# A transformer block of eight stages on one core: the order of the last products of a stage, of the first products of the next, and of a weight split between them

## What is computed

```python
# first block
x = x + g1 * short_conv_mixer(modulate(rmsnorm(x, norm1_g), sh1, sc1), ...)
x = x + g2 * swiglu(modulate(rmsnorm(x, norm2_g), sh2, sc2), ffn_w_in, ffn_w_out)
x = rmsnorm(x, final_g)
# second block, for l in 0, 1
h = _swiglu(_rmsnorm(x, g[0]), w_gate[l, 0], w_up[l, 0], w_down[l, 0])
x = x + 0.5 * _rmsnorm(h, g[1])
h = _rmsnorm(x, g[2])
h = _mixer_even(h, ...) if l % 2 == 0 else _mixer_odd(h, ...)   # conv + window attention / forgetting attention
x = x + _rmsnorm(h, g[3])
h = _swiglu(_rmsnorm(x, g[4]), w_gate[l, 1], w_up[l, 1], w_down[l, 1])
x = x + 0.5 * _rmsnorm(h, g[5])
```

## Time and profile before

| | us |
|---|---|
| median of 3 runs (lowest, highest) | 1375.23 (1374.13, 1375.32) |
| profiled execution, whole | 1372.25 |
| its span, first to last instruction | 1370.5 |
| TensorE busy (share) | 1292.2 (94%) |
| VectorE busy | 832.8 (61%) |
| ScalarE busy | 670.5 (49%) |
| GpSimd busy | 156.8 (11%) |
| mean granted TensorE clock | 0.988 of full |

### The profile page before, as it was taken

How to read it: one execution, slowest core, us unless ns; L and a number is a source line. 1 busy time by engine, 2 the same in 40 slices (tenths; PEclk the granted TensorE clock), 3 DMA queues, 4 the chain that set the end, 5 groups by cost and what they waited for, 6 DMA issues and landing times.

```text
span 1370.5 us, 18389 instructions
## 1 busy us (share of the span) xinstructions
PE 1292.2 (94%) x6757; PEld 1079.7 (79%) x6757; DVE 832.8 (61%) x1015; ACT 670.5 (49%) x993; POOL 156.8 (11%) x121
## 2 busy tenths in 40 slices
PE   2969899999899999899999999999999999999997
PEld 1859688888688888786788888888888798788886
DVE  5998664454655555755655556655555577655554
ACT  2304444444555445555644456654445665644453
POOL 1880393000600000200000000000000100000000
PEclk9989999999999999999999999999999999999999
DMA  9967565555255556371465555555563433365551
GB/s 341 346 229 266 189 230 194 188 184 200 93 185 189 191 191 225 102 234 63 138 218 184 184 199 184 183 186 184 184 214 123 154 140 123 118 220 184 184 199 61
DMA packets 171452, 253.62 MB, mean 185 GB/s; under 512 B 9657, under 2 KB 135821, under 8 KB 171405
## 3 DMA queue, kind: packets, MB, share of 16 engines
q1 hardware_dynamic: 168208, 244.33, 52.7%
q0 software_dynamic: 2304, 8.41, 1.6%
q10 hardware_dynamic: 894, 0.25, 0.1%
HBM read 249.76 MB, written 1.05 MB: 183 GB/s over the span
## 4 chain that ended last, share of the span: by engine, by line
PE 84%; DVE 10%; ACT 3%; issue 1%; DMA 1%; POOL 0%; DVEq 0%; SPq 0%; ACTq 0%; POOLq 0%
PE ps L514 26%; PE ps L516 26%; PE ps L515 26%; DVE tmp L1572 2%; PE ps L556 2%; DVE w_lo L1369 2%; PE ps L816 1%; DVE x_sb L1425 1%; DVE tmp L1522 1%; DVE tmp L1420 1%; PE ps L534 1%; PE ps L711 1%; DMA raw<-in_ada_w 1%; PE ps L700 1%; ACT xn L1010 1%
## 5 line engine op out<-in xcount | busy, mean ns | idle before, releaser
L514 PE MATMUL ps<-w_lo,xT_hi 128*128 128x512 f32 x944 | 376.3, 399 | 4.8 <-DVE xT_lo L1450 2.7
L516 PE MATMUL ps<-w_hi,xT_lo 128*128 128x512 f32 x944 | 369.9, 392 | 0.0
L515 PE MATMUL ps<-w_hi,xT_hi 128*128 128x512 f32 x944 | 369.3, 391 | 0.0
L1369 DVE TENSOR_TENSOR w_lo<-raw,w_hi 128x2048 fp32r<-128x2048 f32 x117 | 278.0, 2378 | 150.0 <-ACT w_hi L988 150.0
L1374 DVE SCALAR_TENSOR_TENSOR w_lo<-raw,par,w_hi 128x512 fp32r<-128x512 f32 x336 | 230.4, 747 | 139.7 <-ACT w_hi L993 139.6
L988 ACT ACTIVATE w_hi<-raw 128x2048 fp32r<-128x2048 f32 x117 | 223.5, 1912 | 179.1 <-PE ps L516 154.3
L993 ACT ACTIVATE w_hi<-raw,par 128x512 fp32r<-128x512 f32 x336 | 214.4, 711 | 0.8 <-PE ps L516 0.8
L514 PEld LDWEIGHTS ps<-w_lo,xT_hi 128*128 128x128 f32 x944 | 178.6, 189 | 42.2 <-DVE xT_lo L1450 3.0
L516 PEld LDWEIGHTS ps<-w_hi,xT_lo 128*128 128x128 f32 x944 | 178.0, 189 | 38.2
L515 PEld LDWEIGHTS ps<-w_hi,xT_hi 128*128 128x128 f32 x944 | 178.5, 189 | 35.6 <-issue 0.2
L514 PE MATMUL ps<-w_lo,hT_hi 128*128 128x512 f32 x400 | 156.5, 391 | 0.0
(11 more groups left out here) (212 smaller groups left out, 1388.6 us busy)
## 6 DMA issues: line engine op xcount, KB each, us to landing
raw<-in_ffn_w_gate SPq DMA_DIRECT2D x88, 512.0 KB, 3.7
raw<-in_ffn_w_up SPq DMA_DIRECT2D x88, 512.0 KB, 4.7
raw<-in_ffn_w_down SPq DMA_DIRECT2D x88, 512.0 KB, 4.0
raw<-in_ffn_w_in SPq DMA_DIRECT2D x44, 512.0 KB, 4.5
raw<-in_conv_w_in SPq DMA_DIRECT2D x24, 512.0 KB, 5.1
raw<-in_fox_w_in SPq DMA_DIRECT2D x24, 512.0 KB, 4.6
raw<-in_ffn_w_out SPq DMA_DIRECT2D x22, 512.0 KB, 4.0
raw<-in_ada_w SPq DMA_DIRECT2D x16, 512.0 KB, 6.7
```

The lines of the kernel that those rows point to most:

```text
L514: pe.matmul(o, a_hi, b_lo, start=first, stop=False, skip_group_check=True)
L515: pe.matmul(o, a_hi, b_hi, start=False, stop=False, skip_group_check=True)
L516: return pe.matmul(o, a_lo, b_hi, start=False, stop=last, skip_group_check=True)
L1369: dve.tensor_tensor(w_lo[:, slot_of(n), :], raw[:, slot_of(n), :], w_hi[:, slot_of(n), :].bitcast(F32), ALU.subtract).then_inc(raw_done, 1)
```

## The change

It has six parts.
1. **Last products**: first tokens go through the last two units, then second tokens (all FFN stages, AB; in CONV over units 14 and 15, with the row product behind them; in FOX half of unit 14 for second tokens stays ahead of unit 15 for first tokens).
2. **First products** (`first_units`, `fresh_hi`, `fresh_lo`): for each unit the eight matmuls with high x come first and wait for ScalarE alone, then the four with low x. The second tokens are transposed after the high products of unit n + 1. In FFN stages both transposes use banks 2 and 3 (`turn_bank`), so the second one waits for the low part of the first.
3. **The late split** (`quarter`) is issued on ScalarE behind the root of the first tokens, and on VectorE behind the first residual.
4. **Fillers**: `WARM_NORMED` is 6 and stands only ahead of AB and FOX; all others go.
5. **Table load** of the square root after AB and FOX: earlier on ScalarE.
6. After FFN0 the final norm (`final_x`) is a step of its own; at FFN0 the wait for the shift row moves to its use.

The diff, cut to its core (ScalarE's and VectorE's lists are shown for the borders only):

```diff
-WARM_TURNED, WARM_FOLDED, WARM_FINAL, WARM_NORMED = 4, 5, 12, 18
+WARM_NORMED = 6
...
+        def turn_bank(s, t, h):
+            return 2 + h if s in FFNS else 2 * t + h
...
+                    if s in FFNS and t == 1:
+                        pe.wait_ge(xT_ok, 4 * s + h + 1)
...
+            def fresh_hi(s, n, h, t, bank):
+                hi, lo = unit(n)
+                pe.wait_ge(xT_hi_ok, 4 * s + 2 * t + h + 1)
+                for k in range(4):
+                    c = slice(k * 512, (k + 1) * 512)
+                    x_k = xT_hi[:, 4 * h + k, tok(t)]
+                    pe.matmul(ps[:, bank, :], x_k, lo[:, c], start=h == 0 and k == 0, stop=False, skip_group_check=True)
+                    pe.matmul(ps[:, bank, :], x_k, hi[:, c], start=False, stop=False, skip_group_check=True)
+            def fresh_lo(s, n, h, t, bank):
+                hi, _ = unit(n)
+                pe.wait_ge(xT_ok, 4 * s + 2 * t + h + 1)
+                for k in range(4):
+                    mm = pe.matmul(ps[:, bank, :], xT_lo[:, 4 * h + k, tok(t)], hi[:, k * 512:(k + 1) * 512], start=False,
+                                   stop=h == 1 and k == 3, skip_group_check=True)
+                return mm
+            def first_units(s, banks):
+                n = BASE[s]
+                turn_x(s, 0)
+                fresh_hi(s, n, 0, 0, banks[0])
+                fresh_lo(s, n, 0, 0, banks[0])
+                fresh_hi(s, n + 1, 1, 0, banks[0])
+                turn_x(s, 1)
+                mm = fresh_lo(s, n + 1, 1, 0, banks[0])
+                if s in FFNS:
+                    mm.then_inc(up_tok0, 1)
+                fresh_hi(s, n, 0, 1, banks[1])
+                fresh_lo(s, n, 0, 1, banks[1]).then_inc(w_used, 1)
+            def second_unit(s, bank):
+                fresh_hi(s, BASE[s] + 1, 1, 1, bank)
+                fresh_lo(s, BASE[s] + 1, 1, 1, bank).then_inc(w_used, 1)
...
-                down_part(last - 1, hT_hi, hT_lo, 0, 1, False, False).then_inc(w_used, 1)
                 pe.wait_ge(hT_ok, NCH * (f + 1))
                 down_part(last, yT_hi, yT_lo, 0, 0, False, True).then_inc(y_tok0, 1)
+                down_part(last - 1, hT_hi, hT_lo, 0, 1, False, False).then_inc(w_used, 1)
                 down_part(last, yT_hi, yT_lo, 0, 1, False, True).then_inc(w_used, 1)
...
-            for i in range(4):
+            for i, tk in ((0, 0), (0, 1), (1, 0), (1, 1), (2, 0), (3, 0), (2, 1), (3, 1)):
...
+            out_part(14, 1, ks=(0,))
             out_part(15, 0)
+            out_part(14, 1, ks=(1,))
             out_part(15, 1)
... ScalarE, in between(b)
-                if b not in FFNS:
-                    warm_up(ACT.Sqrt)
...
+                if b == CONV:
+                    before(0)
+                    for k in range(4):
+                        quarter(n, k)
                     turned_hi(s, 0)
-                    after(1)
-                    before(0)
-                    split(BASE[s] + 2)
+                    before(1)
+                    split(n + 1)
                     turned_hi(s, 1)
-                    before(1)
                 elif s in NORMED:
                     after(0)
+                    for k in range(3):
+                        quarter(n, k)
                     before(0)
                     after(1)
                     turned_hi(s, 0)
+                    quarter(n, 3)
                     before(1)
-                    split(BASE[s] + 2)
+                    split(n + 1)
                     turned_hi(s, 1)
+                elif s in FOLDED:
+                    after(0)
+                    for k in range(3):
+                        quarter(n, k)
+                    if b == FFN0:
+                        turned_hi(s, 0)
+                        quarter(n, 3)
+                    else:
+                        quarter(n, 3)
+                        turned_hi(s, 0)
+                    after(1)
+                    before(0)
+                    split(n + 1)
+                    turned_hi(s, 1)
+                    before(1)
... ScalarE, stage AB
+            warm_up(ACT.Sqrt)
             split(n + 10)
             split(n + 11)
-            split_late(n + 12)
             between(AB, ACT.Silu)
... VectorE, in between(b)
-                if s < 8:
-                    split_piece(BASE[s] + 1, (0, 1, 2))
                 residual(b, 0)
-                if s < 8:
-                    split_piece(BASE[s] + 1, (3,))
-                if s in FOLDED:
+                if b == CONV:
+                    norm_x(s, 0)
+                    residual(b, 1)
                     turned_lo(s, 0)
+                    split_piece(n, (0, 1, 2, 3))
+                    norm_x(s, 1)
+                    turned_lo(s, 1)
...
+                elif b == FFN0:
+                    final_x(0)
+                    residual(b, 1)
+                    turned_lo(s, 0)
+                    split_piece(n, (0, 1, 2, 3))
+                    final_x(1)
+                    rms_x(x_event(s), 0)
+                    turned_lo(s, 1)
+                    rms_x(x_event(s), 1)
+                elif s in FOLDED:
+                    split_piece(n, (0, 1, 2))
+                    turned_lo(s, 0)
+                    split_piece(n, (3,))
                     residual(b, 1)
                     rms_x(x_event(s), 0)
                     turned_lo(s, 1)
                     rms_x(x_event(s), 1)
```

120 lines of the change are left out of this document (48 added, 72 removed).

## The result

The changed kernel takes 1349.32 us (median of 4 runs, 1347.51 to 1351.19); the kernel before, measured beside it, 1374.87 (1374.13 to 1375.32). The ratio is 0.982, 95% interval 0.9805 to 0.9836: 25.5 us less, 1.8%. Profiled execution against profiled execution it is 1372.25 to 1350.36, 21.9 us. The forecast was 19.9 us of gain and 1355.3.

What follows compares the result with a forecast made beforehand. TensorE was taken as the bound, with 62 us of loss at seven stage borders. Border gains less the end's 0.35 and 3.1 for clock gave 19.9 us: 1352.35 profiled, plus 3.0 for the median, 1355.3; range 1348.8 to a little above 1363.

Steps and rivals of the forecast that it cites:

- the end: End of the program: the output hangs on the second tokens, which come 0.35 us later by the new wait.
- The walk with durations of before: Stage borders: step-by-step timing of the engines in the new order with old-trace durations; 0.9 us won at FFN2 to FFN3.
- the hidden product at FFN3: FFN2 to FFN3: third unit's bank is freed by VectorE's hidden product, behind a split and two copies; wait some 1.7 us.
- FOX's unit 15: FOX to FFN4: unit 15 for first tokens needs the last head's low part from VectorE; new wait of 1.26 us.
- normalised x: FFN1 to AB and FFN3 to FOX: TensorE's remaining pause for normalised x, 1.05 us.
- one factor of 1.3 on all of VectorE's work: First two borders: GpSimd beside VectorE stretches its work by 1.3, taken as halfway, leaving gains of 4.6 and 3.7 us.
- two falls: First two borders: new pauses lower the granted clock once at each, costing 1.55 us apiece, 3.1 us together.
- rival 4: First two borders: no GpSimd stretch and no clock fall; 26.4 us won, 1348.8 us; chance 0.15.
- 1 (the clock falls at the other borders): Other five borders: the clock falls there too, since 138 of 162 fillers go; 7.8 us, 1363 us; chance 0.16.
- 2 (late second unit): Five more borders: second unit comes late, each 2 us; 10 us less won, 1365 us; chance 0.10.
- 3: First two borders: GpSimd stretches all of VectorE's work; 1358.2 us; chance 0.10.
- 5: Seven borders: low clock for long, 8 us at each, 28 us lost, slower at 1380 us; chance 0.04.

Runs made afterwards that it cites:

- e7: Changed kernel with FOX's gate-column copies behind FFN3's first hidden product, and the last FOX head's low part ahead of the split of FFN4's first unit: 1345.81 us.
- e8: Changed kernel with GpSimd's work at the first two borders started later, behind the transposes of FFN0's and FFN1's second tokens: 1344.6 us.
- e9: Changed kernel with the square root's table load again behind the last splits of AB and FOX, just ahead of the first root: 1354.35 us in one run.
- e2: Changed kernel where products with high x wait for the low part too, their order kept: 1362.87 us, ratio 0.9927.
- e12: The kernel before with none of its 162 fillers, else unchanged: 1379.21 us, ratio 1.0041.
- e4: Changed kernel with the late unit split ahead of the first root and residual again: 1386.43 us, ratio 1.0093.

## Why the prediction was right, point by point

| border | won, forecast | won, measured |
|---|---|---|
| CONV to FFN0 | 4.6, less 1.55 for the clock | 5.3 |
| FFN0 to FFN1 | 3.7, less 1.55 | 3.15 |
| FFN1 to AB | 3.6 | 3.6 |
| AB to FFN2 | 4.8 | 4.6 |
| FFN2 to FFN3 | 0.9 | 1.15 |
| FFN3 to FOX | 3.6 | 3.6 |
| FOX to FFN4 | 2.1 | 2.1 |
| the end | -0.35 | -0.35 |

- **The walk with durations of before** gave five borders to 0.25 us. The waits it named are in the timeline where it put them: 1.03 us for the hidden product at FFN3 (1.7 forecast), 1.00 at FOX's unit 15 (1.26), 0.87 to 0.88 for normalised x (1.05), none ahead of the transposes of FFN2, FFN3 and FFN4. Ahead of the last unit the starts are 0.49 us apart in four FFNs and 0.59 in FFN0 where a product takes 0.23, so 0.26 to 0.36 (0.35). The third units come 24.53, 26.13 and 24.18 us behind the start (24.8, 26.1 and 24.0). e7 prices the first two by experiment (1.19 and 1.26 us). One reading in the walk is off without effect: the pause of 2.5 us at AB to FFN2 is 2.36 in the trace (659.80).
- **The first two borders.** With no stretch the walk ends at 28.9 and 27.7 us (35.02 - 6.1 and 33.29 - 5.6); e8, which takes GpSimd away, measured 29.08 and 27.46. So the range was right, but the picture behind it, one factor of 1.3 on all of VectorE's work, was not: in the changed kernel the quarters at CONV have their own length (2.49) and one normalisation hasn't (1.87), and in e9 it is the other way about. A sum of single meetings would have been the term, and no row of before could give it for the new order. At CONV to FFN0 the measured 29.68 is 0.8 over the walk without any stretch, at FFN0 to FFN1 28.59 at full clock is 0.9 over it.
- **The clock was the mis-sized term.** I charged 3.1 us for two falls, as if the pauses decided it. The profile shows one fall, at FFN0 to FFN1, of 3.5 us, which cost 1.55; none at CONV to FFN0, with pauses of 1.74 and 1.19. In the other direction FOX's old wait was followed by 6.8 us of low clock in place of 3.4, 1.4 us that nothing in the change makes. Before the change 13.8 us of the border windows were at half clock (0.10 x 2 x 35.02 + 0.05 x 2 x 33.29 + 0.06 x 2 x 28.78); now 3.6. So up to 5 of the 23.5 us won are clock and 18 are waits.
- **Table load.** I gave the earlier load a part of AB's 4.8 us. e9 shows that it earns nothing there: the quarters' move behind the root had already opened the gap. The sum wasn't hurt, since the walk counted the chain and not the parts.
- **Profiled execution and median.** I added 3.0 us for the median. The four spans of the changed kernel are 1345.7 to 1349.5 with mean clocks of 0.992 to 0.990. A difference of 0.002 of 1348 us is 2.7 us of time lost to low clock, most of their spread. So the offset belonged to one execution of before and not to the kernel: after, the profiled execution lies 1.0 above the median. Without the offset the forecast would have been 1352.35, against 1350.36 profiled. The offset also moved the range's low end to 1348.8, and the measured median is only 0.5 us inside it; that it is inside at all is in part luck. That 1349.32 is so near rival 4's number is luck too: a stretch and a fall were both there.
- **What cancelled.** With their clock terms the borders and the end were forecast at 19.9 us and won 23.15, 3.3 more, nearly all at the first two. Outside them 1.15 us were lost that no term had (0.86 later at the first border, 1.4 in FOX, less 1.1 in AB). So the 2 us between forecast and profile are smaller than the errors in it.
- **Not foreseen**: 1.1 us won inside AB, by GpSimd's additions, which meet a low part of VectorE's elsewhere in the new order (3.66 us in place of 5.46).
- **Not tested**: part 4 but for its last 24 fillers (no run puts the others back into the changed kernel), part 6, and the order of products in part 2, of which e2 undoes the wait alone.
- **Rivals.** 1 (the clock falls at the other borders): not there, because the pauses had gone; e12 shows that it was real for pauses of the old length. 2 (late second unit): only at the first two borders, as in the walk. 3 and 4: the chip lay between. 5: e4 shows its mechanism, 41 us at the lower clock and a kernel slower than before, when one part is left out, though half of that loss is waits.

## What to carry to other kernels

Walk the border between two stages engine by engine with durations of the old trace; where no third engine works beside the queues this was good to 0.25 us here, and it tells which two edits only pay together. Then price the pauses that stay twice, with and without a stretch of half clock behind each, and judge small edits by the windows that they touch, since a low stretch elsewhere moves the total by 1.4 to 2.8 us. Where another engine works beside a critical queue and isn't needed yet, start it later: that took 0.6 and 1.1 us off two borders here, the clock apart.
